# Keys transposed by VectorE instead of TensorE in tiles 1 to 3, diagonal sums moved inside a unit, first loads issued later

## The chip, the core and the metric

The kernel runs on one NeuronCore of a Trainium2 chip. The metric is the device time of one execution in microseconds; the time before is the median of three runs. One execution was profiled, and all rows shown come from it.

## What is computed

One encoder layer over 2048 positions of 1024 channels, in float32. What matters here is its HGRN2 branch: a gated linear recurrence with 4 heads, a 128 x 128 state each, computed chunk by chunk.

```python
h = _rmsnorm(x, mix_norm[l]);  z = h @ w_in[l]
u, v, q, f, i, og, gates = _split_cols(z, IN_SIZES)
...
forget = lb + (1.0 - lb) * sigmoid(ff);  g_log = log(max(forget, TINY));  k = (1.0 - lb) * sigmoid(-ff)
# per chunk, G = cumsum(g_log):
A = einsum('bhid,bhijd,bhjd->bhij', q, decay, k)
o = einsum('bhij,bhje->bhie', A, v) + einsum('bhid,bhde->bhie', q * exp(G), state)
state = exp(G_last) * state + einsum('bhjd,bhje->bhde', k * exp(G_last - G), v)
...
x = x + y @ w_out[l];  x = x + _conv_ffn(_rmsnorm(x, ffn_norm[l]), ...);  return _rmsnorm(x, final_norm)
```

## The kernel before

**Tiling.** The positions are cut into four tiles `t` of 512 (`TT`), each tile into four chunks of 128. Channels lie in the partitions. Weights come in units of 128 output columns; every fp32 product is done as three fp32r products (high weight by high input, high by low, low by high), so that a unit over the eight input blocks is 24 matmuls of 128x512 in `products` (lines 1165, 1166 and 1172). `from_h` is such a unit on the normalised input. In tile 0 each weight unit is loaded raw, split by ScalarE and VectorE (`weights_lo`, line 800), and written out; later tiles load the split units.

**A head.** In each tile, a loop over four heads `h` runs on each engine, and each engine works through its own instructions in the order of the code; semaphores (the `Steps` objects, where `did` counts a step and `at` names the count to wait for) tie them. On TensorE a head is: four units (forget gate, query, gate a, output gate); `level(1)`, two fp32 matmuls of the pair scores at distance 1; two fp32r matmuls with the matrix of ones (lines 1346 and 1348), which sum the diagonal scores into bank 4 and end step `s1`; a fifth unit (gate b); `flip`, four fp32 transposes of the decayed keys `kp` into bank 2 (line 1237, three in the last tile, whose last state is not needed); the levels 2 to 64, twelve fp32 matmuls (line 1245), whose ends are the steps `s2_4`, `s8_16` and `s32_64`; the sixth unit; then the state update (line 1364, keys by token times values), the output products (lines 1369 and 1373) and the mixer (line 1378). Before the update TensorE waits for step `m64` of VectorE, for `k_tok` of ScalarE and for `i_head`.

**VectorE in a head** builds the keys (`kp`, ended by `kl128`) and queries (`qp`, ended by `qp128`, line 931) of all levels, then copies the scores under masks out of PSUM into `scores`: level 1, diagonal, and levels 2 to 64 (lines 941 and 945), each copy behind a wait and a one-element memset (line 939). The last copy is `m64`. It goes on with the first state (line 946), the normalised values `v_head` (line 949) and, when the update is there, the four steps of the state (line 957), for each of which TensorE waits at line 1373. ScalarE copies the flipped keys from bank 2 to `k_tok` (line 619) behind the fifth unit.

**The start.** SP issues all loads in the order of its code: parameters, the first piece of x, the two halves of the first weight unit (line 360, semaphore `half_unit_in`, and line 361), three more pieces of x, the second unit (line 363), the last four pieces, the identity. TensorE first runs 13 warm-up products (line 1297). ScalarE makes the high parts: piece 0 of x, both halves of unit 0 (lines 532 and 534), piece 1 of x, then unit 1 (line 528); VectorE makes the low parts of x (line 784).

Of the kernel before, what the change touches and what calls it, by code (L numbers as in the profile page):

```python
# [6 lines left out]
ACT = mybir.ActivationFunctionType  # L7
ALU = mybir.AluOpType

P = 128  # L10
# [6 lines left out]
NH = 4  # L17
# [105 lines left out]
def build(nc, x_t, w_units, par, masks_in, ident_in, gm_wt, ln_b, gm_bs, out):  # L123
# [145 lines left out]
    N_CONST = 16 * 3  # L269

    tok_act = Steps(sem("tok_act"), ["v0", "v1"] + [f"i{c}" for c in range(NC)])
    head_act = Steps(sem("head_act"), ["i_head", "sig_f", "sig_q", "qk_hi", "sig_og", "k_tok", "o_sq", "sq_hi", "o_rms"])
    head_pe = Steps(sem("head_pe"), ["s1", "k_tok", "s2_4", "s8_16", "s32_64", "update", "o", "mix", "o_sum"])
    names = ["forget", "floor", "qk", "qp1", "qr1"]
    for s in LEVELS:
        names += (["qk_lo"] if s == 16 else []) + [f"kc{s}", f"kl{2 * s}", f"t{2 * s}"]
    for s in LEVELS:
        names += ([f"qr{s}"] if s > 1 else []) + [f"qp{2 * s}"]
    head_dve = Steps(sem("head_dve"), ["k"] + names
                     + ["m1", "m0", "m2", "m4", "m8", "m16", "m32", "m64", "st0"] + [f"vh{c}" for c in range(NC)] + ["st1", "st2", "st3", "st4",  # L280
                        "mix", "sq_lo", "a", "a_hi", "a_lo", "inv", "unit", "b", "b_hi", "b_lo"])
    ln_dve = Steps(sem("ln_dve"), [f"bn{c}" for c in range(NC)] + [f"ag{c}" for c in range(NC)] + ["inv"])
    ln_act = Steps(sem("ln_act"), ["std"])
    mix_dve = Steps(sem("mix_dve"), [f"{n}{j}" for j in range(2) for n in ("b", "a", "y", "y_hi", "y_lo")], 1)
# [69 lines left out]
    def _(sp):  # L354
# [59 lines left out]
        load_x(0, 0)  # L414
        load_raw(0)
        load_x(0, 1)
        load_x(0, 2)
        load_x(0, 3)
        load_raw(1)
# [62 lines left out]
    def _(act):  # L482
# [68 lines left out]
        for t in range(0, NT):  # L551
# [44 lines left out]
            for h in range(0, NH):  # L596
                it = t * NH + h
                u = h * 6
                act.wait_ge(*tok_act.at(f"i{NC - 1}", t))
                act.activation(blocks(i_head[:, :], P), i_tok[:, :, bass.ts(h, P)],  # L600
                               ACT.Copy).then_inc(*head_act.did("i_head"))
                unit_behind(t, U_HEAD, u)
                act.activation(sig_f[:, :], bank[0][:, :], ACT.Sigmoid).then_inc(*head_act.did("sig_f"))
                act.activation(sig_nf[:, :], bank[0][:, :], ACT.Sigmoid, scale=-1.0).then_inc(evac[0], 1)
                unit_behind(t, U_HEAD + 1, u)
                act.activation(sig_q[:, :], bank[1][:, :], ACT.Sigmoid).then_inc(*head_act.did("sig_q"))
                act.wait_ge(*head_dve.at("qk", it))
                act.activation(qk_hi[:, :], qk[:, :], ACT.Copy).then_inc(*head_act.did("qk_hi"))
                unit_behind(t, U_HEAD + 2, u)
                if h == 0 and t:  # L610
                    act.wait_ge(out_sent, t * 16 * KD)
                act.activation(gate_a_head[:, h, :], bank[0][:, :], ACT.Sigmoid).then_inc(evac[0], 1)
                unit_behind(t, U_HEAD + 3, u)
                act.activation(sig_og[:, :], bank[1][:, :], ACT.Sigmoid).then_inc(*head_act.did("sig_og"))
                unit_behind(t, U_HEAD + 4, u)
                act.activation(gate_b_head[:, h, :], bank[0][:, :], ACT.Sigmoid).then_inc(evac[0], 1)
                act.wait_ge(*head_pe.at("k_tok", it))
                tokens = (NC - (t == NT - 1)) * P
                act.activation(k_tok[:, 0:tokens], bank[2][:, 0:tokens], ACT.Copy).then_inc(*head_act.did("k_tok"))
                unit_behind(t, U_HEAD + 5, u)  # L620
                act.activation(u_act[:, h, :], bank[1][:, :], ACT.Gelu).then_inc(evac[1], 1)
                act.wait_ge(*head_pe.at("o", it))
                act.activation(head_o[:, :], bank[4][:, :], ACT.Square).then_inc(*head_act.did("o_sq"))
                act.wait_ge(*head_act.at("o_sq", it))
                act.activation(sq_hi[:, :], head_o[:, :], ACT.Copy).then_inc(*head_act.did("sq_hi"))
                act.wait_ge(*head_pe.at("o_sum", it))
                act.activation(head_o[:, :], bank[5][:, :], ACT.Sqrt, bias=eps[:, 0:1],
                               scale=1.0 / P).then_inc(*head_act.did("o_rms"))
# [90 lines left out]
    def _(dve):  # L719
# [121 lines left out]
        for t in range(0, NT):  # L841
# [25 lines left out]
            for h in range(0, NH):  # L867
# [62 lines left out]
                    then(f"qr{s}")  # L930
                    dve.tensor_tensor(q_r, queries(s), spread(t_l, s), ALU.mult).then_inc(*head_dve.did(f"qp{2 * s}"))

                for n, (s, made, before) in enumerate(((1, "s1", f"qp{P}"), (0, "s1", "m1"), (2, "s2_4", "m0"),
                                                       (4, "s2_4", "m2"), (8, "s8_16", "m4"), (16, "s8_16", "m8"),
                                                       (32, "s32_64", "m16"), (64, "s32_64", "m32"))):
                    dve.wait_ge(*zero_dve.at("scores", t))
                    dve.wait_ge(*head_pe.at(made, it))
                    then(before)
                    dve.memset(scratch[:, n:n + 1], 0.0)
                    if s:  # L940
                        dve.copy_predicated(half_of(scores[:, :], s, True),
                                            mask_of[s].rearrange("p (a n s) -> p a n s", a=2, s=s),
                                            level_out(s).rearrange("p (a n s) -> p a n s", a=2, s=s)).then_inc(*head_dve.did(f"m{s}"))
                    else:
                        dve.copy_predicated(scores[:, :], mask_of[0], bank[4][:, :]).then_inc(*head_dve.did("m0"))
# [210 lines left out]
    def _(pe):  # L1156
# [142 lines left out]
        for t in range(0, NT):  # L1299
# [26 lines left out]
            def o_sum(h):  # L1326
# [3 lines left out]
                pe.wait_ge(*head_dve.at("sq_lo", t * NH + h))  # L1330
                pe.matmul(bank[5][:, :], ones_r[:, :], sq_lo[:, :], start=False, stop=True).then_inc(*head_pe.did("o_sum"))

            for h in range(0, NH):
                it = t * NH + h
                u = h * 6
                used = t * B_TILE + h * 3 + B_HEAD
                from_h(t, U_HEAD, u, 0, used, within=o_sum if h else None, of=h - 1)
                from_h(t, U_HEAD + 1, u, 1, used)
                from_h(t, U_HEAD + 2, u, 0, used + 1)
                from_h(t, U_HEAD + 3, u, 1, used + 1)  # L1340
                pe.wait_ge(*tok_act.at(f"i{NC - 1}", t))
                pe.wait_ge(*head_dve.at("qr1", it))
                pe.wait_ge(*head_dve.at("kc1", it))
                level(1)
                pe.wait_ge(*head_act.at("qk_hi", it))
                pe.matmul(bank[4][:, :], ones_r[:, :], qk_hi[:, :], start=True, stop=False)
                pe.wait_ge(*head_dve.at("qk_lo", it))
                pe.matmul(bank[4][:, :], ones_r[:, :], qk_lo[:, :], start=False, stop=True).then_inc(*head_pe.did("s1"))
                from_h(t, U_HEAD + 4, u, 0, used + 2)
                pe.wait_ge(*head_dve.at(f"kl{P}", it))  # L1350
                flip(bank[2], kp, NC - (t == NT - 1)).then_inc(*head_pe.did("k_tok"))
                for a, b in ((2, 4), (8, 16), (32, 64)):
                    pe.wait_ge(*head_dve.at(f"qr{a}", it))
                    level(a)
                    pe.wait_ge(*head_dve.at(f"qr{b}", it))
                    level(b).then_inc(*head_pe.did(f"s{a}_{b}"))
                from_h(t, U_HEAD + 5, u, 1, used + 2)
                pe.wait_ge(*head_dve.at("m64", it))
                pe.wait_ge(*head_act.at("k_tok", it))
                pe.wait_ge(*head_act.at("i_head", it))  # L1360

                for c in range(NC - (t == NT - 1)):
                    cols = slice(c * P, (c + 1) * P)
                    mm = pe.matmul(bank[2][:, cols], k_tok[:, cols], i_head[:, cols], start=True, stop=True)  # L1364
                mm.then_inc(*head_pe.did("update"))
                for c in range(NC):
                    cols = slice(lain(c) * P, (lain(c) + 1) * P)
                    none_yet = t == 0 and c == 0
                    mm = pe.matmul(bank[4][:, cols], i_head[:, cols], scores[:, cols], start=True, stop=none_yet)  # L1369
                    if none_yet:  # L1370
                        continue
                    pe.wait_ge(*head_dve.at(f"st{c}", it))
                    mm = pe.matmul(bank[4][:, cols], state[:, c, :], qp[:, cols], start=False, stop=True)  # L1373
                mm.then_inc(*head_pe.did("o"))

                for c in range(NC):
                    cols = slice(c * P, (c + 1) * P)
                    mm = pe.matmul(bank[3][:, cols], v_head[:, cols], gm_w[:, h, :], start=True, stop=True)  # L1378
                mm.then_inc(*head_pe.did("mix"))
# [201 lines left out]
```

## Time and profile before

| | us |
|---|---|
| median of 3 runs | 2819.47 |
| lowest, highest | 2819.13, 2820.02 |
| profiled execution, its own time | 2818.25 |
| its span | 2816.4 |
| TensorE busy | 2805.1 (100% of the span) |
| TensorE weight load busy | 2340.2 (83%) |
| VectorE busy | 1562.7 (55%) |
| ScalarE busy | 745.3 (26%) |
| GpSimd busy | 123.0 (4%) |

The granted TensorE clock is full speed in all 40 slices of the span. "PE" is TensorE's matmul side, "PEld" its weight loads, DVE VectorE, ACT ScalarE, POOL GpSimd, SP the engine that issues the loads. Matmuls overlap: a record of 128x512 lasts 0.39 us, while the next one starts 0.227 us after it, so the time that a stretch takes on TensorE is read from start to start. An fp32 matmul leaves two records.

### The profile page before, as it was taken

How to read it: one execution, taken by the hardware profiler on the slowest of the kernel's cores; microseconds unless marked ns; L12 is line 12 of the kernel's file. 1: busy time of each engine (PE TensorE's matmuls, PEld its weight loads, DVE VectorE, ACT ScalarE, POOL GpSimd, SP SyncE). 2: the span in 40 equal slices, each digit the busy share in tenths (PEclk: the TensorE clock that was granted, in tenths of full speed). 3: DMA queues.
4: the chain of work that ended last, by engine and by line, in shares of the span. 5: the costliest groups of instructions: out<-in, count | busy, mean ns of one | idle time of the engine just before them, and what ended most of it. 6: DMA issues, size and time to landing. Idle time of an engine off the chain costs nothing.

```text
span 2816.4 us, 32878 instructions
## 1 busy us (share of the span) xinstructions
PE 2805.1 (100%) x12934; PEld 2340.2 (83%) x12934; DVE 1562.7 (55%) x3044; ACT 745.3 (26%) x1021; POOL 123.0 (4%) x72
## 2 busy tenths in 40 slices
PE   9999999999999999999999999999999999999998
PEld 8888888888888888888888888888888888888887
DVE  6995777756377345553347734555334772555521
ACT  5433344433132113221123201222112220222200
POOL 1003400024000000000000000000000000000000
PEclk9999999999999999999999999999999999999999
DMA  8678888889644555556564455555656445555555
GB/s 313 231 245 280 299 292 290 291 322 319 242 148 163 191 212 194 195 194 233 208 224 147 159 197 207 194 194 194 237 211 215 157 151 212 200 193 192 194 207 177
DMA packets 123739, 614.58 MB, mean 218 GB/s; under 512 B 13987, under 2 KB 16337, under 8 KB 76096
## 3 DMA queue, kind: packets, MB, share of 16 engines
q1 hardware_dynamic: 122688, 610.50, 61.3%
q8 instruction: 103, 1.69, 0.2%
q0 software_dynamic: 896, 1.97, 0.2%
q14 instruction: 52, 0.43, 0.0%
HBM read 474.00 MB, written 138.41 MB: 217 GB/s over the span
## 4 chain that ended last, share of the span: by engine, by line
PE 99%; DVE 1%; DMA 0%; ACT 0%; issue 0%; SPq 0%; DVEq 0%
PE bank L1165 29%; PE bank L1166 29%; PE bank L1172 29%; PE bank L1245 2%; PE bank L1232 2%; PE bank L1230 2%; PE bank L1231 2%; PE bank L1373 1%; PE bank L1279 1%; PE bank L1364 1%; PE bank L1378 1%; PE bank L1369 1%; PE bank L1288 0%; PE bank L1285 0%; PE bank L1181 0%; PE bank L1178 0%
## 5 line engine op out<-in xcount | busy, mean ns | idle before, releaser
L1165 PE MATMUL bank<-h_hi,w_both 128*128 128x512 f32 x2400 | 937.1, 390 | 0.0
L1166 PE MATMUL bank<-h_lo,w_both 128*128 128x512 f32 x2400 | 934.5, 389 | 0.0
L1172 PE MATMUL bank<-h_hi,w_both 128*128 128x512 f32 x2400 | 593.4, 389 | 0.0
L1172 PEld LDWEIGHTS bank<-h_hi,w_both 128*128 128x128 f32 x2400 | 450.5, 188 | 93.4
L1165 PEld LDWEIGHTS bank<-h_hi,w_both 128*128 128x128 f32 x2400 | 450.7, 188 | 93.1
L1166 PEld LDWEIGHTS bank<-h_lo,w_both 128*128 128x128 f32 x2400 | 450.7, 188 | 93.2
L1055 DVE TENSOR_TENSOR z<-bank,rms_inv 128x512 f32<-128x512 f32 x176 | 121.9, 692 | 340.9 <-PE bank L1172 340.6
L1068 DVE SCALAR_TENSOR_TENSOR conv<-z,params,conv 128x512 f32<-128x512 f32 x352 | 263.7, 750 | 6.2
L1166 PE MATMUL bank<-g_lo,w_both 128*128 128x512 f32 x682 | 265.3, 389 | 0.0
L1165 PE MATMUL bank<-g_hi,w_both 128*128 128x512 f32 x682 | 265.3, 389 | 0.0
L493 ACT ACTIVATE w_both<-raw 128x1024 fp32r<-128x1024 f32 x122 | 129.5, 1061 | 325.7 <-PE bank L1172 277.8
L665 ACT ACTIVATE conv<-z,params 128x512 f32<-128x512 f32 x176 | 143.5, 815 | 178.4 <-DVE z L1055 170.2
L1172 PE MATMUL bank<-g_hi,w_both 128*128 128x512 f32 x682 | 169.7, 389 | 0.0
L1165 PEld LDWEIGHTS bank<-g_hi,w_both 128*128 128x128 f32 x682 | 128.0, 188 | 26.6
L1166 PEld LDWEIGHTS bank<-g_lo,w_both 128*128 128x128 f32 x682 | 128.0, 188 | 26.6
L1172 PEld LDWEIGHTS bank<-g_hi,w_both 128*128 128x128 f32 x682 | 128.0, 188 | 26.6
L1121 DVE TENSOR_TENSOR res<-res,bank 128x512 f32<-128x512 f32 x31 | 21.3, 687 | 231.0 <-PE bank L1172 231.0
L479 POOL TENSOR_TENSOR w_both<-raw,w_both 128x1024 fp32r<-128x1024 f32 x46 | 111.2, 2418 | 551.5 <-ACT w_both L493 536.1
L670 ACT ACTIVATE silu<-conv 128x512 f32<-128x512 f32 x88 | 55.4, 630 | 239.4 <-PE bank L1172 232.6
L800 DVE TENSOR_TENSOR w_both<-raw,w_both 128x1024 fp32r<-128x1024 f32 x78 | 95.4, 1223 | 18.8 <-ACT w_both L493 11.9
L674 ACT ACTIVATE g_hi<-g_f 128x512 fp32r<-128x512 f32 x88 | 55.7, 633 | 151.8 <-DVE g_f L1078 151.8
L1165 PE MATMUL bank<-y_hi,w_both 128*128 128x512 f32 x224 | 87.1, 389 | 0.0
(268 smaller groups left out, 3176.6 us busy)
## 6 DMA issues: line engine op xcount, KB each, us to landing
w_both<-w_split SPq DMA_DIRECT2D x371, 1024.0 KB, 4.8
w_split<-w_both SPq DMA_DIRECT2D x248, 512.0 KB, 5.6
raw<-w_units SPq DMA_DIRECT2D x123, 512.0 KB, 5.3
x_in<-x_t SPq DMA_DIRECT2D x32, 256.0 KB, 5.7
res<-x_t SPq DMA_DIRECT2D x32, 256.0 KB, 5.2
out<-res SPq DMA_DIRECT2D x24, 256.0 KB, 7.1
out<-res SPq DMA_DIRECT2D x16, 128.0 KB, 1.9
w_both<-w_split SPq DMA_DIRECT2D x2, 512.0 KB, 5.6
```

The lines of the kernel that those rows point to most:

```text
L479: po.tensor_tensor(w_lo[j], raw[j][:, :, :], w_hi[j].bitcast(F32), ALU.subtract).then_inc(lo_made, 1)
L493: act.activation(w_hi[slot], raw[slot][:, :, :], ACT.Copy).then_inc(hi_made, 1)
L665: act.activation(conv[j][:, :], z[j][:, 2:TT + 2], ACT.Identity, bias=par_col(C_CB + f + j * KF), scale=par_col(C_CW + 4 * KF + f + j * KF ...
L800: dve.tensor_tensor(w_lo[u % 2], raw[u % 2][:, :, :], w_hi[u % 2].bitcast(F32), ALU.subtract).then_inc(lo_made, 1)
L1055: dve.tensor_tensor(z[j][:, 2:TT + 2], bank[2 * (f % 2) + j][:, :], rms_inv[:, :], ALU.mult).then_inc(evac[j], 1)
L1068: dve.scalar_tensor_tensor(out=conv[j][:, :], in0=z[j][:, tap:TT + tap], scalar=par_col(C_CW + 2 * KF * tap + f + j * KF), in1=conv[j][:, ...
L1165: pe.matmul(dst, w_hi[slot][:, off + k, :], rhs_hi(k), start=first and k == 0, stop=False)
L1166: pe.matmul(dst, w_hi[slot][:, off + k, :], rhs_lo(k), start=False, stop=False)
L1172: mm = pe.matmul(dst, w_lo[slot][:, off + k, :], rhs_hi(k), start=False, stop=last and k == n - 1)
L1230: pe.matmul(dst[c][:, :], hi, w[0], start=k == 0, stop=False)
L1231: pe.matmul(dst[c][:, :], hi, w[1], start=False, stop=False)
L1232: mm = pe.matmul(dst[c][:, :], lo, w[0], start=False, stop=k == KD - 1)
```

## The change

Three things are altered.

1. In tiles 1 to 3 the transposes of `kp` are made by VectorE: 16 block transposes of 32 partitions by four times 32 columns (the four chunks at once) write `k_tok` directly, behind `qp128` and ahead of the masked copies. `flip` on TensorE and the copy on ScalarE remain in tile 0 alone. TensorE's wait for `k_tok` ahead of the update goes to the new semaphores.
2. The two diagonal sums are issued in the middle of the fifth unit (`diagonal`, after the first eight matmuls), and `level(1)` goes behind the fifth unit to the other levels. `s1` now ends with the diagonal alone, so the diagonal copy `m0` comes first on VectorE and level 1 (`m1`) waits for `s2_4`.
3. SP waits for `half_unit_in` after the second piece of x; what follows in its queue (pieces 2 and 3, the second unit, pieces 4 to 7, the identity, and all later transfers) is issued behind that wait.

```diff
@@ SP
         load_x(0, 1)
+
+        sp.wait_ge(half_unit_in, 16)
         load_x(0, 2)
@@ ScalarE, head loop
-                act.wait_ge(*head_pe.at("k_tok", it))
-                tokens = (NC - (t == NT - 1)) * P
-                act.activation(k_tok[:, 0:tokens], bank[2][:, 0:tokens], ACT.Copy).then_inc(*head_act.did("k_tok"))
+                if t == 0:
+                    act.wait_ge(*keys_pe.at("flip", h))
+                    act.activation(k_tok[:, :], bank[2][:, :], ACT.Copy).then_inc(*keys_act.did("k_tok"))
@@ VectorE, head loop
+                if t:
+                    then(f"kl{P}")
+                    for a in range(0, P, 32):
+                        for b in range(0, P, 32):
+                            op = dve.transpose(blocks(k_tok[b:b + 32, :], P)[:, :, a:a + 32], blocks(kp[a:a + 32, :], P)[:, :, b:b + 32])
+                    op.then_inc(*keys_dve.did("k_tok"))
+
-                for n, (s, made, before) in enumerate(((1, "s1", f"qp{P}"), (0, "s1", "m1"), (2, "s2_4", "m0"),
+                for n, (s, made, before) in enumerate(((0, "s1", f"qp{P}"), (1, "s2_4", "m0"), (2, "s2_4", "m1"),
@@ TensorE, head loop
+            def diagonal(h):
+                it = t * NH + h
+                pe.wait_ge(*tok_act.at(f"i{NC - 1}", t))
+                pe.wait_ge(*head_act.at("qk_hi", it))
+                pe.matmul(bank[4][:, :], ones_r[:, :], qk_hi[:, :], start=True, stop=False)
+                pe.wait_ge(*head_dve.at("qk_lo", it))
+                pe.matmul(bank[4][:, :], ones_r[:, :], qk_lo[:, :], start=False, stop=True).then_inc(*head_pe.did("s1"))
...
-                pe.wait_ge(*tok_act.at(f"i{NC - 1}", t))
+                from_h(t, U_HEAD + 4, u, 0, used + 2, within=diagonal, of=h)
+                if t == 0:
+                    pe.wait_ge(*head_dve.at(f"kl{P}", it))
+                    flip(bank[2], kp, NC).then_inc(*keys_pe.did("flip"))
                 pe.wait_ge(*head_dve.at("qr1", it))
                 pe.wait_ge(*head_dve.at("kc1", it))
                 level(1)
-                pe.wait_ge(*head_act.at("qk_hi", it))
-                pe.matmul(bank[4][:, :], ones_r[:, :], qk_hi[:, :], start=True, stop=False)
-                pe.wait_ge(*head_dve.at("qk_lo", it))
-                pe.matmul(bank[4][:, :], ones_r[:, :], qk_lo[:, :], start=False, stop=True).then_inc(*head_pe.did("s1"))
-                from_h(t, U_HEAD + 4, u, 0, used + 2)
-                pe.wait_ge(*head_dve.at(f"kl{P}", it))
-                flip(bank[2], kp, NC - (t == NT - 1)).then_inc(*head_pe.did("k_tok"))
...
-                pe.wait_ge(*head_act.at("k_tok", it))
+                pe.wait_ge(*(keys_dve.at("k_tok", it - NH) if t else keys_act.at("k_tok", h)))
```

TensorE in a head of tile 1, from the end of the fourth unit to the levels, before the change (the fifth unit's other matmuls left out):

```order
L1172 MATMUL bank<-h_hi,w_both_50 128x512 x8
L1245 MATMUL bank<-qr_101,k_first_93 128x2x64 x2
L1346 MATMUL bank<-qk_hi,ones_r 128x512
L1348 MATMUL bank<-qk_lo,ones_r 128x512
...
L1172 MATMUL bank<-h_hi,w_both_51 128x512 x8
L1237 MATMUL bank<-ident,kp 128x128 x4
L1245 MATMUL bank<-qr_102,k_first_94 128x2x64 x2
```

The same place after the change:

```order
L1185 MATMUL bank<-h_hi,w_both_50 128x512 x8
...
L1351 MATMUL bank<-qk_hi,ones_r 128x512
L1353 MATMUL bank<-qk_lo,ones_r 128x512
...
L1185 MATMUL bank<-h_hi,w_both_51 128x512 x8
L1258 MATMUL bank<-qr_101,k_first_93 128x2x64 x2
L1258 MATMUL bank<-qr_102,k_first_94 128x2x64 x2
```

The four transposes (L1237) are gone, the two sums stand within the fifth unit, and level 1 stands beside level 2.

VectorE at the end of the queries in the same head, before the change (L931 is `qp128`, L945 the diagonal copy):

```order
L931 TENSOR_TENSOR qp<-qr_107,total_114 128x2x2x64
L939 MEMSET scratch 128x1
L941 COPY_PREDICATED scores<-masks,bank 128x2x128
L939 MEMSET scratch 128x1
L945 COPY_PREDICATED scores<-masks,bank 128x512
L939 MEMSET scratch 128x1
L941 COPY_PREDICATED scores<-masks,bank 128x2x64x2
```

And after it:

```order
L936 TENSOR_TENSOR qp<-qr_107,total_114 128x2x2x64
L943 STREAM_TRANSPOSE k_tok<-kp 32x4x32 x16
L952 MEMSET scratch 128x1
L958 COPY_PREDICATED scores<-masks,bank 128x512
L952 MEMSET scratch 128x1
L954 COPY_PREDICATED scores<-masks,bank 128x2x128
L952 MEMSET scratch 128x1
L954 COPY_PREDICATED scores<-masks,bank 128x2x64x2
```

Sixteen transposes stand ahead of the copies, and the diagonal and level 1 have changed places.

## Rows read from the trace of the kernel before

**Rows 1.** The page, part 4: the chain that ended last, by engine.

```profile
PE 99%; DVE 1%; DMA 0%; ACT 0%; issue 0%; SPq 0%; DVEq 0%
```

**Rows 2.** Timeline, TensorE, tile 1: start, length, instruction; the segment that changes.

```profile
811.24 1.98 PE L1172 MATMUL bank<-h_hi,w_both 128*128 128x512 f32 x8
...
816.68 1.98 PE L1172 MATMUL bank<-h_hi,w_both 128*128 128x512 f32 x8
818.50 0.60 PE L1245 MATMUL bank<-qr,k_first 128*128 128x128 f32 x4
...
824.87 0.60 PE L1237 MATMUL bank<-ident,kp 128*128 128x128 f32 x4
825.30 2.84 PE L1245 MATMUL bank<-qr,k_first 128*128 128x128 f32 x24
827.90 0.47 PE L1165 MATMUL bank<-h_hi,w_both 128*128 128x512 f32 x1
```

**Rows 3.** The same timeline where two ones products already stand within a unit.

```profile
798.07 0.39 PE L1329 MATMUL bank<-sq_hi,ones_r 128*128 128x512 f32 x1
...
798.53 0.39 PE L1165 MATMUL bank<-h_hi,w_both 128*128 128x512 f32 x1
```

**Rows 4.** Timeline, TensorE, a head of the last tile: the three transposes.

```profile
2179.85 0.49 PE L1237 MATMUL bank<-ident,kp 128*128 128x128 f32 x3
2180.18 2.84 PE L1245 MATMUL bank<-qr,k_first 128*128 128x128 f32 x24
```

**Rows 5.** Timeline, TensorE, tile 1: the update and the second state's product.

```profile
833.45 1.05 PE L1364 MATMUL bank<-i_head,k_tok 128*128 128x128 f32 x8
...
835.01 0.42 PE L1373 MATMUL bank<-qp,state 128*128 128x128 f32 x2
```

**Rows 6.** Timeline, VectorE, the same head; in brackets idle before, and the releaser.

```profile
823.04 0.43 DVE L931 TENSOR_TENSOR qp<-qr,total 128x256 f32<-128x256 f32 x1
823.63 0.74 DVE L941 COPY_PREDICATED scores<-masks,bank 128x256 f32<-128x256 uint32 x1 [0.17 <-DVE qp L931]
...
826.48 0.06 DVE L939 MEMSET scratch<- 128x1 f32 x1 [1.21 <-PE bank L1245]
...
829.79 0.45 DVE L941 COPY_PREDICATED scores<-masks,bank 128x256 f32<-128x256 uint32 x1 [0.16 <-DVE scores L941]
...
830.13 0.22 DVE L946 COPY state<-carry 128x128 f32<-128x128 f32 x1
...
834.54 1.11 DVE L957 SCALAR_TENSOR_TENSOR state<-state,total,bank 128x128 f32<-128x128 f32 x3 [3.16 <-PE bank L1364]
```

**Rows 7.** Groups by line and shape, VectorE, 806 to 836 us: busy us, mean ns.

```profile
L957 DVE SCALAR_TENSOR_TENSOR state<-state,total,bank 128x128 f32<-128x128 f32 x3 | 1.0, 347 | 3.2 <-PE bank L1364 3.2
...
L918 DVE TENSOR_TENSOR total<-total 128x128 f32<-128x128 f32 x1 | 0.3, 284 | 0.0
```

**Rows 8.** Timeline, VectorE, tile 0, second head: the last masked copy.

```profile
132.22 0.45 DVE L941 COPY_PREDICATED scores<-masks,bank 128x256 f32<-128x256 uint32 x1
```

**Rows 9.** Timeline, TensorE, the same head: the update behind that copy.

```profile
132.72 1.16 PE L1364 MATMUL bank<-i_head,k_tok 128*128 128x128 f32 x8
```

**Rows 10.** Timeline of the start, SP, ScalarE and VectorE.

```profile
4.03 0.43 SPq L363 DMA_DIRECT2D raw<-w_units  x1
...
5.17 0.63 ACT L532 ACTIVATE w_both<-raw 128x512 fp32r<-128x512 f32 x1
...
9.09 0.75 DVE L784 SCALAR_TENSOR_TENSOR hx_lo<-x_in,params,hx_hi 128x512 fp32r<-128x512 f32 x1 [3.08 <-ACT hx_hi L524]
...
10.91 1.06 ACT L528 ACTIVATE w_both<-raw 128x1024 fp32r<-128x1024 f32 x1 [0.81 <-DMA raw<-w_units]
```

**Rows 11.** Timeline of the start, TensorE: first unit.

```profile
7.10 0.66 PE L1285 MATMUL bank<-w_both,hx_hi 128*128 128x512 f32 x1
...
9.20 0.47 PE L1285 MATMUL bank<-w_both,hx_hi 128*128 128x512 f32 x1
9.89 0.49 PE L1288 MATMUL bank<-w_both,hx_lo 128*128 128x512 f32 x1 [0.22 <-DVE hx_lo L784]
```

More of the change, by code:

```diff
@@ L271, in build @@
     tok_act = Steps(sem("tok_act"), ["v0", "v1"] + [f"i{c}" for c in range(NC)])
-    head_act = Steps(sem("head_act"), ["i_head", "sig_f", "sig_q", "qk_hi", "sig_og", "k_tok", "o_sq", "sq_hi", "o_rms"])
-    head_pe = Steps(sem("head_pe"), ["s1", "k_tok", "s2_4", "s8_16", "s32_64", "update", "o", "mix", "o_sum"])
+    head_act = Steps(sem("head_act"), ["i_head", "sig_f", "sig_q", "qk_hi", "sig_og", "o_sq", "sq_hi", "o_rms"])
+    head_pe = Steps(sem("head_pe"), ["s1", "s2_4", "s8_16", "s32_64", "update", "o", "mix", "o_sum"])
     names = ["forget", "floor", "qk", "qp1", "qr1"]
@@ L279, in build @@
     head_dve = Steps(sem("head_dve"), ["k"] + names
-                     + ["m1", "m0", "m2", "m4", "m8", "m16", "m32", "m64", "st0"] + [f"vh{c}" for c in range(NC)] + ["st1", "st2", "st3", "st4",
+                     + ["m0", "m1", "m2", "m4", "m8", "m16", "m32", "m64", "st0"] + [f"vh{c}" for c in range(NC)] + ["st1", "st2", "st3", "st4",
                         "mix", "sq_lo", "a", "a_hi", "a_lo", "inv", "unit", "b", "b_hi", "b_lo"])
+    keys_pe, keys_act = Steps(sem("keys_pe"), ["flip"]), Steps(sem("keys_act"), ["k_tok"])
+    keys_dve = Steps(sem("keys_dve"), ["k_tok"])
     ln_dve = Steps(sem("ln_dve"), [f"bn{c}" for c in range(NC)] + [f"ag{c}" for c in range(NC)] + ["inv"])
```

## The prediction

> **What bounds the kernel now.** I read the chain of waits first: it is TensorE for 99% of the span [rows 1], so the time changes only by what TensorE executes and by how long it stands still. What the change takes off VectorE or ScalarE is worth nothing by itself, and what it puts there is free as long as TensorE doesn't wait. The next view is the timeline of a head of tile 1, on TensorE [rows 2, 5] and on VectorE [rows 6]. The reader is to see who is early there. VectorE waits 1.21 us for the levels and 3.16 us for the update [rows 6]; TensorE reaches the update at 833.45 [rows 5], while the last masked copy was over at 829.79 + 0.45 = 830.24 [rows 6]. That is a slack of about 3 us, and 1.2 us more within VectorE's wait for the levels. All other heads of tiles 1 to 3 repeat this pattern to a few hundredths. Against this slack stand the 16 new transposes.
>
> **What TensorE is spared.** The segment from the end of the fourth unit to the start of the sixth takes 827.90 - 818.50 = 9.40 us [rows 2]. Afterwards it holds one unit, two ones products and fourteen level matmuls. A unit takes 816.68 - 811.24 = 5.44 us [rows 2]. Two ones products within a unit take 798.53 - 798.07 = 0.46 us [rows 3]. Fourteen level matmuls leave 28 records, as the four transposes (4 records) and twelve levels (24) do now: 827.90 - 824.87 = 3.03 us [rows 2]. The sum is 8.93, so a head gains 0.47 us: 0.43 for the transposes (825.30 - 824.87) and 0.04 for one change less between fp32 and fp32r products. In the last tile only three transposes go, 2180.18 - 2179.85 = 0.33 us [rows 4], and the gain is 0.37. Eight heads by 0.47 and four by 0.37 make **5.24 us**. ScalarE's copy also goes; it lay beside TensorE's work and counts nothing. Level 1 comes later than before; its copy on VectorE now waits for `s2_4`. Today's wait for that step ends 826.48 - 825.30 = 1.18 us after the levels' start [rows 2, 6]; the new levels start at 818.50 + 5.44 + 0.46 = 824.40, with level 1 (0.22) ahead, so the step is there at 825.8, while VectorE with the transposes and the diagonal copy ahead gets to it only at about 829.5.
>
> **What VectorE gets.** No transpose by VectorE is in this trace, so the time T from one to the next has to be bounded. The work is 4 by 32 = 128 elements in each partition. A tensor_tensor of 128 elements takes 284 ns and the scalar_tensor_tensor of line 957 347 ns [rows 7]. Two instructions without a wait overlap: the state copy starts at 830.13 while the copy ahead of it ends at 830.24 [rows 6], so 0.11 us. Three dependent ones at line 957 take 1.11 us [rows 6], a gap of (1.11 - 3 x 0.347) / 2 = 0.035 us between end and start. T thus lies between 0.284 - 0.11 = 0.17 and 0.347 + 0.035 = 0.38 us. I choose within this: each transpose writes another block of 32 partitions than the one before, and no row shows two such instructions overlapping, so I take them one after another, 0.284 + 0.035 = 0.32. A block can also leave only when its 32 columns are in; at (0.43 - 0.284) / 128 = 0.00114 us an element [rows 6, 7] that is up to 0.036 us more, 0.355. I take **T = 0.33 us**, 5.28 us a head.
>
> The Trainium skill has a price of its own. "VectorE: DVE Perf Modes", section "The three transpose paths", gives 311 ns for a VectorE transpose of 128x128 bf16. An estimate from it with the gap above is T = 0.346, and the loss below would be 14 us instead of 11. The same page, "Two Vector instructions with no wait between them", holds an instruction until all earlier ones have finished when its input or output starts in another group of 32 partitions than the last one's. By that rule all sixteen run one after another, which speaks against this change; no row here can show it.
>
> **What lies behind the transposes.** Queued behind them on VectorE are all masked copies, `v_head` and the state. The last query product starts at 823.04, and the next instruction without a wait can start 0.32 later, at 823.36. The copies take 823.63 to 826.48 less the wait of 1.21, which is 1.64, then 0.16 for the semaphore between two copies, then 826.48 to 830.24, which is 3.76 [rows 6]: 5.56 us. The last copy then ends at 828.92 + 16T. TensorE arrives at 833.45 - 0.47 = 832.98. Tile 0 shows the case in which TensorE is late for this very reason: the copy ends at 132.67 [rows 8], the update starts 0.05 later [rows 9] and takes 1.16 instead of 1.05 us [rows 5, 9], since its weights were not loaded ahead. So no stall arises while 16T is under 832.98 - 0.05 - 828.92 = 4.01 us, **T under 0.25 us**. Above it the stall is 16T - 4.01 + 0.11. The state behind it can't make it up: the second state's product already lasts 0.42 rather than 0.39 us [rows 5], directly behind the state's steps. With T = 0.33 the stall is 1.38 us a head, 1.28 in the last tile, where TensorE comes 0.10 later. Less the gain, a head loses 0.91, and twelve heads **10.9 us**. A stall doesn't grow from head to head, as VectorE's next head begins with TensorE's units.
>
> **Tile 0.** The transposes stay. The 0.04 us of the changed order is worth up to 0.2 in four heads, but where the update already waits for the last copy [rows 8, 9] it is lost. I take 0.1.
>
> **The start.** TensorE begins at 7.10, when its warm-up ends; the half unit is there by 5.17 [rows 10, 11], so an earlier half unit brings nothing. Then TensorE stands from 9.20 + 0.23 = 9.43 to 9.89 for the low part of piece 1 [rows 10, 11]. With fewer transfers beside it, piece 1 and the second half come earlier, worth up to 0.46 us. Against it, all that follows in SP's queue moves: the second unit was issued at 4.03 and is now issued behind the wait and two pieces, at about 6. Its arrival (just before 10.91 [rows 10]) ended a wait of ScalarE, and pieces 2 and 3 of x are worked on behind it. If it comes as much later as it is issued, 2 us, up to 1.5 us of that reach TensorE. As the transfers until then share the same bandwidth, I take a small gain of 0.2; bounds -0.46 and +1.5.
>
> **Sum.** 2818.25 (the profiled execution's own time; the span of 2816.4 and 1.85 around it) + 10.9 - 0.1 - 0.2 = 2828.85. The median is 1.22 above the profiled execution: 2830.1.
>
> **The rivals.**
>
> - *The transposes overlap and fit* (T under 0.25). For it speaks that most neighbours on VectorE do overlap and that a plain 128-element operation of 284 ns less 0.11 would leave T at 0.17. Against it, the change of partitions at each step. Then the whole gain stands: 2819.47 - 5.24 - 0.3 = 2813.9, faster by 0.2%. This is the case on the other side; it decides at T = 0.25.
> - *They just miss* (T from 0.25 to 0.30). The stall of 0.1 to 0.9 us a head eats the gain: at T = 0.27 stall and gain are equal, and the time is 2819.
> - *Much slower transposes*, for instance two cycles for a 4-byte element: T = 0.33 + 128 x 0.00114 = 0.48, stall 3.8, loss 3.3 a head, 2859. Nothing in the profile speaks for it but that every VectorE row is of another kind.
> - *The start decides.* If the second unit comes 2 us late, 1.5 us are lost once. It shifts each case by that and no more.
>
> **How the numbers follow.** My forecast, VectorE late at the last copy with T between 0.30 and 0.38, has 0.58; overlapping and fitting 0.20; just missing 0.15; much slower 0.07. The predicted time is 2830. In its own case T from 0.30 to 0.38 gives a loss of (16T - 3.90 - 0.47) x 12, 5.2 to 20.5 us, or 2824.5 to 2840. The fitting case with a start at its better end reaches 2813.5. The range 2813.5 to 2840 leaves out the slow case and the edges. A measurement of this kernel can tell about 0.2% (5.6 us) from no change. The fitting case lies just at that bound, so it gives 0.12 to faster and the rest to the same; the near miss is the same, with 0.01 of faster; of my forecast 0.04 falls below 5.6 us. Faster 0.13, same 0.26, slower 0.61.
>
> **What would show it.** In the profile after: between the fifth and sixth unit one block of level matmuls of 3.03 us and no transposes; the ones products 0.46 us within the fifth unit; sixteen transposes a head, 0.33 us from start to start, 5.3 in all; VectorE no longer waiting for the levels, and hardly for the update; the update on TensorE about 0.05 us behind the last masked copy, some 1.3 us behind the sixth unit's end; a head of tile 1 0.9 us longer than now; no wait at line 1288's place at the start. If the update follows the sixth unit without a gap, T was under 0.25 and the forecast is wrong by its main term. A granted clock below full speed behind the new stalls would make the loss larger; nothing here shows that, as the clock is full in every slice.

## The result: 2832.5 us, 0.47% slower

The changed kernel takes 2832.53 us (median of 6 runs, 2831.41 to 2833.33) against 2819.30 for the kernel before on the same chip. The ratio is 1.0047, with a 95% interval of 1.0037 to 1.0057. The forecast was 2830, with a range of 2813.5 to 2840. The profiled execution took 2831.75 us, its span is 2830.0: 13.6 more than before. Of all executions in this document one, in the run called control, took 3111 us at a granted clock of 0.85, and it counts in no ratio; the others had 0.998 or 0.999.

The page after, busy time by engine and the chain that ended last:

```profile
PE 2804.2 (99%) x12890; PEld 2334.3 (82%) x12890; DVE 1620.2 (57%) x3236; ACT 739.5 (26%) x1009; POOL 123.0 (4%) x72
```

```profile
PE 86%; DVE 11%; issue 1%; DMA 1%; ACT 0%; POOL 0%; DVEq 0%; SPq 0%; POOLq 0%; ACTq 0%
```

VectorE, at 1% of the chain before [rows 1], now has 11%. Its busy time rose by 57.5 us, while the span rose by 13.6. TensorE's waits name the place. The view lists who waited for whom: us in total, times, longest.

```profile
PE bank L1382 <- DVE scores L954: 13.2, 12, 1.4
PE bank L1310 <- DVE ones L766: 1.5, 1, 1.5
PE bank L1298 <- ACT hx_hi L529: 1.2, 1, 1.2
```

L1382 is the state update, L954 a masked copy: twelve waits, one for each head of tiles 1 to 3. The third row is the start. Neither is there before; the second row is, at line 1297.

The timeline of a head of tile 1 after the change, TensorE; it answers to [rows 2, 5]:

```profile
819.20 1.98 PE L1185 MATMUL bank<-h_hi,w_both 128*128 128x512 f32 x8
821.01 0.39 PE L1178 MATMUL bank<-h_hi,w_both 128*128 128x512 f32 x1
...
822.83 0.39 PE L1351 MATMUL bank<-qk_hi,ones_r 128*128 128x512 f32 x1
...
825.12 1.98 PE L1185 MATMUL bank<-h_hi,w_both 128*128 128x512 f32 x8
826.93 3.29 PE L1258 MATMUL bank<-qr,k_first 128*128 128x128 f32 x28
829.98 0.48 PE L1178 MATMUL bank<-h_hi,w_both 128*128 128x512 f32 x1
...
833.70 1.98 PE L1185 MATMUL bank<-h_hi,w_both 128*128 128x512 f32 x8
837.02 1.16 PE L1382 MATMUL bank<-i_head,k_tok 128*128 128x128 f32 x8 [1.34 <-DVE scores L954]
```

And VectorE in the same head; it answers to [rows 6]:

```profile
825.57 0.43 DVE L936 TENSOR_TENSOR qp<-qr,total 128x256 f32<-128x256 f32 x1
825.91 5.04 DVE L943 STREAM_TRANSPOSE k_tok<-kp 32x128 f32<-32x128 f32 x16
831.01 0.06 DVE L952 MEMSET scratch<- 128x1 f32 x1
831.09 0.73 DVE L958 COPY_PREDICATED scores<-masks,bank 128x512 f32<-128x512 uint32 x1
831.98 0.06 DVE L952 MEMSET scratch<- 128x1 f32 x1 [0.17 <-DVE scores L958]
832.33 0.74 DVE L954 COPY_PREDICATED scores<-masks,bank 128x256 f32<-128x256 uint32 x1 [0.29 <-issue]
...
836.52 0.44 DVE L954 COPY_PREDICATED scores<-masks,bank 128x256 f32<-128x256 uint32 x1 [0.16 <-DVE scores L954]
```

From the end of the fourth unit to the start of the sixth it is 829.98 - 821.01 = 8.97 us, 0.43 less than the 9.40 before. The last eight matmuls of a unit take 1.81 us (819.20 to 821.01), so the sixth unit ends at 833.70 + 1.81 = 835.51. The last masked copy ends at 836.52 + 0.44 = 836.96, and the update starts at 837.02, 0.06 behind it. The sixteen transposes take from 825.91 to 831.01, 5.10 us or 0.319 each, the pause behind the last one included. The waits of 1.21 and 3.16 us that VectorE had [rows 6] are gone. In this head a further 0.35 us lies between the memset at 831.98 and its copy at 832.33, of which the row puts 0.29 down to "issue": nothing that the profile shows was waited for. Such a gap falls into this stretch in three of the twelve heads, whose wait is 1.34 to 1.37 us; in the other nine it is 1.01 or 1.02.

The start, after the change: the issue of the second unit, ScalarE's wait for it, and TensorE's wait for the high part of the third piece of x, which ScalarE makes behind that unit [rows 10, 11]:

```profile
5.98 0.43 SPq L366 DMA_DIRECT2D raw<-w_units  x1
```

```profile
11.85 1.06 ACT L533 ACTIVATE w_both<-raw 128x1024 fp32r<-128x1024 f32 x1 [3.14 <-DMA raw<-w_units]
```

```profile
13.66 0.47 PE L1298 MATMUL bank<-w_both,hx_hi 128*128 128x512 f32 x1 [1.17 <-ACT hx_hi L529]
14.36 0.50 PE L1301 MATMUL bank<-w_both,hx_lo 128*128 128x512 f32 x1 [0.22 <-DVE hx_lo L789]
```

The unit is issued 1.95 us later and worked on 0.94 us later. The wait within the first unit is gone, a longer one ahead of the second has come, and the first update stands at 92.60 instead of 91.54, 1.06 later.

**Where the 13.6 us are.** Read in this one execution, the update of the first head stands 1.06 us later than before, that of the last head of tile 0 1.04 later (216.14 against 215.10), that of the very last head 13.04 later (2322.91 against 2309.87). So the start costs 1.06, tile 0 nothing, and the stretch with the twelve heads of tiles 1 to 3 costs 12.0. That includes one new wait of 0.3 us for weights. Such a wait, 0.3 to 1.2 us long, is in five of the twelve profiles, with the change and with its parts taken back.

### The profile page after: what moved, and what is told of

Same layout as the page of the kernel before. It is cut to its first block, busy times and chain, and to the rows that moved or that the text cites. A ratio compares the mean times of both kernels' runs of the same rounds, so it can differ in the third digit from the quotient of the medians.

```text
span 2830.0 us, 32986 instructions
## 1 busy us (share of the span) xinstructions
PE 2804.2 (99%) x12890; PEld 2334.3 (82%) x12890; DVE 1620.2 (57%) x3236; ACT 739.5 (26%) x1009; POOL 123.0 (4%) x72
## 4 chain that ended last, share of the span: by engine, by line
PE 86%; DVE 11%; issue 1%; DMA 1%; ACT 0%; POOL 0%; DVEq 0%; SPq 0%; POOLq 0%; ACTq 0%
PE bank L1178 25%; PE bank L1179 25%; PE bank L1185 25%; DVE k_tok L943 2%; PE bank L1243 2%; PE bank L1245 2%; PE bank L1244 2%; DVE scores L954 1%; DVE qp L936 1%; DVE kp L921 1%; DVE k_first L919 1%; DVE qr L930 1%; PE bank L1382 1%; PE bank L1391 1%; PE bank L1396 1%
## 5 line engine op out<-in xcount | busy, mean ns | idle before, releaser
L805 DVE TENSOR_TENSOR w_both<-raw,w_both 128x1024 fp32r<-128x1024 f32 x78 | 95.4, 1224 | 19.2 <-ACT w_both L498 13.6
L1179 PE MATMUL bank<-y_lo,w_both 128*128 128x512 f32 x224 | 87.2, 389 | 0.0
```

The lines of the kernel that those rows point to most:

```text
L805: dve.tensor_tensor(w_lo[u % 2], raw[u % 2][:, :, :], w_hi[u % 2].bitcast(F32), ALU.subtract).then_inc(lo_made, 1)
L1179: pe.matmul(dst, w_hi[slot][:, off + k, :], rhs_lo(k), start=False, stop=False)
```

## The experiments

My theory was that VectorE ends the last masked copy too late, and nothing else matters but the start. The rivals were the start, the new order of diagonal and level 1, and the new wait or semaphores whatever the transposes take.

**The start undone.**

```diff
         load_x(0, 1)
-
-        sp.wait_ge(half_unit_in, 16)
         load_x(0, 2)
```

> The change without its third part: SP issues all loads without the wait for half_unit_in. Theory (VectorE late at the last masked copy, start a side matter): in the profile of the changed kernel the product that opens the head stage stands 1.06 us later than before, so this run gains 1.0 to 1.1 us on it: span about 2829.0, time about 2831.5, and the stall ahead of each update (1.01 us of idle, 12 times) stays. Rival (the start is a main part of the loss, because all later transfers move): 2827 or less.

Measured: 2830.76 us (ratio 1.0041, 1.0026 to 1.0056), span 2829.2. The first update stands at 91.37 us, 1.23 earlier than with the change, but this execution has a wait of 1.2 us for weights at 713.10, ahead of the heads of tile 1, where the changed kernel's has 0.3. The twelve waits for the scores are 13.2 us, as in the changed kernel. The start is a small part of the loss, as expected.

**The start alone.**

```diff
@@ kernel before
         load_x(0, 1)
+        sp.wait_ge(half_unit_in, 16)
         load_x(0, 2)
```

> The kernel before with SP's wait for half_unit_in behind the second piece of x, nothing else. Theory: the second unit's arrival is late, TensorE waits about 1.2 us for its high part and saves 0.46 at the second block of the first unit: the first head's products stand 1.0 to 1.1 us later, span 2817.4, time about 2820, which a ratio cannot tell from no change. Rival (the later transfers bring back what the start loses, or make it larger): first head's products within 0.3 us of before, or over 2 us later.

Measured: 2820.19 us, ratio 1.0006 (0.9997 to 1.0015), which is no difference by itself; the span is 2818.2. In the trace the first update is at 92.62, and the wait at the second unit is there:

```profile
PE bank L1287 <- ACT hx_hi L526: 0.8, 1, 0.8
```

So the trace shows 1.08 us of loss at the first update; the remaining 0.8 of the span lie later and are not traced to a cause. They are less than the scatter of one kernel: the kernel before took 2817.81 to 2819.89 us beside this run.

The size of the loss scatters too. Four profiles have the late issue and the wait for `m64` ahead of the first update (the changed kernel, this run, and the two with fewer and with in-place transposes below): there the second unit lands between 11.33 and 12.06 us, and the first update stands at 91.91 to 92.75. Four have the issue of before and the same wait: 10.70 to 10.89, and 91.37 to 91.54. The start costs 0.4 to 1.4 us, always a loss.

**The order alone.** The transposes stay on TensorE, ScalarE's copy stays, the start is that of before.

```diff
@@ changed kernel, start undone
-                if t == 0:
-                    act.wait_ge(*keys_pe.at("flip", h))
-                    act.activation(k_tok[:, :], bank[2][:, :], ...)
+                act.wait_ge(*keys_pe.at("flip", it))
+                act.activation(k_tok[:, 0:tokens], bank[2][:, 0:tokens], ...)
-                if t:
-                    ... 16 x dve.transpose(...)
-                if t == 0:
-                    ...
-                    flip(bank[2], kp, NC)
+                flip(bank[2], kp, NC - (t == NT - 1))
```

> The second part of the change alone: diagonal sums within the fifth unit, level 1 behind it, diagonal copy first; the transposes stay on TensorE and the copy on ScalarE in all tiles, the start is that of before. Theory: 0.04 us less a head in tiles 1 to 3 and nothing in tile 0, 0.5 us in all: span about 2815.9, time 2819, no idle of TensorE ahead of the update in tiles 1 to 3. Rival (the later copy of level 1 makes the last masked copy late): TensorE idles ahead of the update and the time is 2822 or more.

Measured: 2819.02 us, ratio 0.9997 (0.9987 to 1.0007). TensorE has no wait ahead of the updates of tiles 1 to 3. The span is 2817.3 instead of the expected 2815.9. Two updates of tile 1, one head apart:

```profile
833.71 1.05 PE L1371 MATMUL bank<-i_head,k_tok 128*128 128x128 f32 x8
```

```profile
874.59 1.05 PE L1371 MATMUL bank<-i_head,k_tok 128*128 128x128 f32 x8
```

A head takes 40.88 us, and 40.84 before (874.29 - 833.45). The rival falls, and my gain of 0.04 us a head falls with it: moving the two sums into the unit and level 1 to the other levels is worth nothing that these runs can tell.

**Ten transposes instead of sixteen.** Two transposes of all 128 partitions and eight of 32; half of the key blocks stay in their own rows.

```diff
-                    for a in range(0, P, 32):
+                    for a in (64, 96):
+                        op = dve.transpose(blocks(k_tok[:, :], P)[:, :, a:a + 32], blocks(kp[:, :], P)[:, :, a:a + 32])
+                    for a in (0, 32):
                         for b in range(0, P, 32):
```

> The changed kernel with 10 transposes a head instead of 16: two of all 128 partitions and eight of 32, which leaves half of the key blocks unmoved, so the states are not the reference's. Theory (slack of 4.0 us a head, 0.319 us a transpose): 3.2 us fit, TensorE doesn't wait ahead of the update and the gain of the removed transposes shows in full, less the 1.06 us of the start: span about 2812.3, time about 2815. Rival (the loss hangs on the new semaphore path or the order, not on the time that the transposes take): time stays near 2832.

Measured: 2815.35 us, ratio 0.9987 (0.9978 to 0.9996), span 2813.8. No wait for the scores is left in TensorE's list. The transposes of a head:

```profile
824.88 0.50 DVE L942 STREAM_TRANSPOSE k_tok<-kp 128x128 f32<-128x128 f32 x2
825.30 2.47 DVE L945 STREAM_TRANSPOSE k_tok<-kp 32x128 f32<-32x128 f32 x8
827.83 0.06 DVE L954 MEMSET scratch<- 128x1 f32 x1
```

They take 2.95 us, within the 4.0 that are free. The first and the last update of tile 1 are at 794.10 and 915.26, so a head takes 40.39 us; before, 792.62 and 915.12 give 40.83. The removed transposes of TensorE are worth 0.45 us a head in tile 1. The loss in the heads hangs on the time that VectorE's transposes take; the new semaphores are still there and make TensorE wait nowhere.

**Sixteen transposes that stay in their rows.** Same size and count, but each writes the 32 partitions that it reads, and four in turn work on the same 32; the keys are not put in their right places.

```diff
-    op = dve.transpose(blocks(k_tok[b:b + 32, :], P)[:, :, a:a + 32], blocks(kp[a:a + 32, :], P)[:, :, b:b + 32])
+    op = dve.transpose(blocks(k_tok[a:a + 32, :], P)[:, :, b:b + 32], blocks(kp[a:a + 32, :], P)[:, :, b:b + 32])
```

> The changed kernel with its 16 transposes of the same size and count, but each writes the 32 partitions that it reads (four in turn on each group of 32), so the blocks are transposed without being moved; the recurrence's states are then not the reference's. Theory 1 (a transpose waits for the one ahead because it writes another group of partitions): within a group they overlap like other neighbours, about 0.20 us from start to start, 12 of 16; the sixteen take about 3.7 us instead of 5.1, which fits into the slack of 4.0: time 2815 to 2817. Theory 2 (0.32 us is what a transpose takes wherever it writes): 5.1 us, time unchanged at 2832.

Measured: 2815.82 us, ratio 0.9988 (0.9979 to 0.9997), span 2813.1, no wait for the scores.

```profile
824.01 3.57 DVE L943 STREAM_TRANSPOSE k_tok<-kp 32x128 f32<-32x128 f32 x16
827.64 0.06 DVE L952 MEMSET scratch<- 128x1 f32 x1
```

Sixteen take 3.63 us here and 5.10 in the changed kernel, for the same work. The durations of the same head in both, minimum, median and maximum in ns, first this run and then the changed kernel:

```profile
L943 DVE STREAM_TRANSPOSE k_tok<-kp x16: 256/260/307, 824.0 to 827.3; 32x128 f32<-32x128 f32 x16
```

```profile
L943 DVE STREAM_TRANSPOSE k_tok<-kp x16: 292/302/309, 825.9 to 830.6; 32x128 f32<-32x128 f32 x16
```

Two neighbours of this run, one by one:

```profile
824.23 0.26 DVE L943 STREAM_TRANSPOSE k_tok<-kp 32x128 f32<-32x128 f32 x1
```

```profile
824.43 0.26 DVE L943 STREAM_TRANSPOSE k_tok<-kp 32x128 f32<-32x128 f32 x1
```

A transpose that follows one in the same rows is recorded with about 260 ns, and the next such one starts 0.193 us after it, before it has ended. One whose rows are not those of the one before is recorded with about 302 ns and starts 0.013 or 0.014 us after the end of that one; in the changed kernel the steps from start to start are 0.305 to 0.320 us. This run has three such changes among its sixteen, the changed kernel fifteen. The difference of 1.47 us a head decides the sign, and it is what separates the forecast from its main rival; for twelve instructions it is 0.12 us each.

The single records also say what "change" means. In the changed kernel the input stays in the same 32 partitions for four transposes and only the output moves, and the steps are the same. The four blocks that stay in place (every fifth of the sixteen) are no exception. So what counts is that the output's rows differ from those of the instruction before, not that a block moves from one group to another. The Trainium skill has the rule in "VectorE: DVE Perf Modes", section "Two Vector instructions with no wait between them": an instruction whose input or output starts in another group of 32 partitions than the last one's is held until all earlier ones have finished. The two runs agree with it.

**The wait moved behind the update.**

```diff
-                pe.wait_ge(*head_dve.at("m64", it))
                 pe.wait_ge(*(keys_dve.at("k_tok", it - NH) if t else keys_act.at("k_tok", h)))
                 ... update ...
+                pe.wait_ge(*head_dve.at("m64", it))
                 ... output products ...
```

> The changed kernel with one line moved: TensorE waits for the last masked copy (m64) behind the state update instead of ahead of it; the update doesn't read the scores. Theory (VectorE's chain itself is the bound: last copy, then v_head for 1.11 us, then the state): the update runs about 1.16 us earlier, but the state still starts when v_head ends, and the second state's product comes at most 0.1 us earlier: gain 0 to 1.2 us in all, time 2831 to 2832.5. Rival (the place of the wait is the cause, and the 0.9 us of the update can be hidden): 12 x 0.9 = 10 us less, 2822.

Measured: 2829.14 us, ratio 1.0036 (1.0022 to 1.0050), span 2827.2: 2.8 us less than the changed kernel, not 0 to 1.2, and far from 10. The waits have moved:

```profile
PE bank L1391 <- DVE state L970: 5.5, 12, 0.5
PE bank L1387 <- DVE scores L954: 2.8, 7, 0.5
```

L1391 is a product with the state, L1387 one with the scores. TensorE comes to the update early and then waits for VectorE twice. The bound is VectorE's chain, not the place of the wait: the rival of 10 us falls. I had the state start when `v_head` ends in both kernels; in the changed kernel it waited for the late update, and started 1.25 us after the end of the last masked copy (838.21 - 836.96), here 1.06 (836.66 - 835.60). That is 0.2 us a head in tiles 1 and 2, next to nothing in tile 3, and 1.5 us in all. The rest of the 2.8 us is not the heads of tiles 1 to 3: 0.4 lie at the start of this execution, 0.6 in tile 0, where the line was moved too, and 0.3 is the wait for weights, which this execution doesn't have.

**Slack made, in all tiles.** `v_head` is computed ahead of the wait for `sig_q`, where VectorE idles; TensorE does the mixer products first, then the update, then waits for `m64`; the sums of squares stand two input blocks later.

```diff
@@ VectorE
                 weights_lo(t, next_lo)
+                ... v_head ...
                 dve.wait_ge(*head_act.at("sig_q", it))
@@ TensorE
                 from_h(t, U_HEAD + 5, u, 1, used + 2)
-                pe.wait_ge(*head_dve.at("m64", it))
+                pe.wait_ge(*head_dve.at("m1", it))
+                ... mixer products ...
                 ... update ...
+                pe.wait_ge(*head_dve.at("m64", it))
                 ... output products ...
```

> The changed kernel with the slack made: v_head is computed on VectorE ahead of the wait for sig_q (1.14 us of idle there), TensorE does the mixer products first, then the update, and waits for m64 only ahead of the output products; the sums of squares stand two input blocks later in the next unit. Theory: the transposes (5.1 us) are then covered, TensorE doesn't idle in the heads of tiles 1 to 3, and the removed transposes show: 0.43 us by 8 and 0.33 by 4 less than before, the start costs 1.06, and tile 0 no longer waits for m64 (up to 1 us): span 2811.5 to 2813, time 2814.5 to 2816. Rival (VectorE is late elsewhere as well, at the state or at the next head): over 2820.

Measured: 2823.07 us, ratio 1.0014 (1.0005 to 1.0023), span 2819.9.

> As the one before (v_head early, mixer first, m64 ahead of the output products), with the start of the kernel before. Theory: another 1.06 us less: span 2810.5 to 2812, time about 2814, ratio to before 0.998. Rival (the early start of loads matters no more once the rest is moved): same as with the changed start.

Measured: 2820.98 us, ratio 1.0008 (0.9999 to 1.0017), span 2818.5. This second run has the start of before. Both missed by 6 us and more: my rival was right that VectorE is late elsewhere, though not at the places that it named. In the run with the start of before, TensorE's waits in tile 1 are down to one of 0.2 us, and there is a new one in tile 0:

```profile
PE bank L1257 <- DVE qr L932: 3.5, 4, 1.1
```

L1257 is a level matmul. In tile 0 VectorE also makes the low parts of the weights and has no idle ahead of `sig_q`, so `v_head` there makes the queries late for the levels. The last update of tile 0 stands at 220.71 us instead of 215.10; 0.9 of that are the mixer products now ahead of it, so tile 0 has become 4.7 us longer.

**Control: the same order with TensorE's transposes.**

> Control: the same reordering (v_head early, mixer first, m64 ahead of the output products, start of before), but with the key transposes left on TensorE and the copy on ScalarE. Theory: only the waits of tile 0 for m64 go, up to 1 us: span 2815.5 to 2816.5, so that the difference to the run with VectorE's transposes is 4.8 us (8 x 0.43 + 4 x 0.33). Rival (the reordering itself makes the gain): within 1 us of the run with VectorE's transposes.

Measured: 2824.23 us, ratio 1.0018 (1.0009 to 1.0027), span 2822.9, with the same 3.4 us of waits for queries in tile 0 and one of 1.1 us for weights. The span is 4.4 us above the run with VectorE's transposes, 3.3 without that one wait. The reordering by itself gains nothing; what gain there is comes from taking the transposes off TensorE.

**Slack made in tiles 1 to 3 only**, tile 0 in the order of the changed kernel, start of before.

```diff
@@ VectorE
+                if t:
+                    values()          # v_head
                 dve.wait_ge(*head_act.at("sig_q", it))
@@ TensorE
+                if t:
+                    pe.wait_ge(*head_dve.at("m1", it))
+                    mixer(it, h)
+                else:
+                    pe.wait_ge(*head_dve.at("m64", it))
                 ... update ...
+                if t:
+                    pe.wait_ge(*head_dve.at("m64", it))
```

> VectorE's transposes with the slack made in tiles 1 to 3 only (v_head ahead of the wait for sig_q, mixer first, m64 awaited ahead of the output products, sums of squares two blocks later), while tile 0 keeps the order of the changed kernel; start of before. In the run that reordered all tiles TensorE had no gap in tile 1 but waited 3.5 us for queries in tile 0, where VectorE has no idle. Theory: those waits go, and what is left is the gain of the removed transposes, 8 x 0.43 + 4 x 0.33 = 4.8 us: span 2811 to 2812.5, time 2813.5 to 2815, ratio to before 0.998. Rival (the new order costs something in tiles 1 to 3 too): 2817 or more.

Measured: 2816.18 us, ratio 0.9991 (0.9982 to 1.0000), span 2813.7. It beats the changed kernel by 16 us, and the kernel before by 3 us, at the edge of what the runs can tell. A head of tile 1, TensorE:

```profile
831.01 1.97 PE L1192 MATMUL bank<-h_hi,w_both 128*128 128x512 f32 x8
832.82 1.05 PE L1358 MATMUL bank<-gm_w,v_head 128*128 128x128 f32 x8
833.71 1.06 PE L1401 MATMUL bank<-i_head,k_tok 128*128 128x128 f32 x8
834.66 0.49 PE L1408 MATMUL bank<-scores,i_head 128*128 128x128 f32 x2
```

The transposes are covered: mixer and update run without a gap. Of the 4.8 us expected, 2.7 came. The output products start 0.95 us after the update instead of 0.89, and their first record lasts 0.49: `m64` still comes a little late. In the last tile, where the update has one matmul less, it is later: the last masked copy, the update and the output products of its third head.

```profile
2267.62 0.44 DVE L963 COPY_PREDICATED scores<-masks,bank 128x256 f32<-128x256 uint32 x1
```

```profile
2267.19 0.83 PE L1401 MATMUL bank<-i_head,k_tok 128*128 128x128 f32 x6
2268.12 0.49 PE L1408 MATMUL bank<-scores,i_head 128*128 128x128 f32 x2
```

The copy ends at 2268.06, and the products start 0.93 us behind the update where they started 0.67 behind it before (2270.03 - 2269.36). Three heads of the last tile lose 0.26 or 0.27 us each in this way, and gain 0.03 instead of 0.33. Over all twelve heads these delays add up to 1.4 us; 0.7 of the missing 2.1 remain untraced.

## Why the prediction was right, point by point

- **The bound and the place.** Right. TensorE waits at the update for the last masked copy, 0.06 us behind its end as tile 0 had shown with 0.05 [rows 8, 9].
- **The transposes' time T.** 0.33 us was assumed and 0.319 measured. That they run one after another, the choice that decided the sign, was right for the reason given: with three changes of rows instead of fifteen, the same sixteen take 0.227 us each, below the limit of 0.25, and there the kernel is faster than before. That the figure is so close is in part luck. Its parts were borrowed from instructions of another kind and missed in opposite directions: 0.284 for the record, which is 0.302, and 0.035 for the pause behind it, which is 0.014.
- **The slack.** 4.01 us was worked out. With T = 0.319 the formula gives a stall of 5.10 - 4.01 + 0.11 = 1.20 us. From the rows, the wait (start of the update less end of the unit) is 1.17 in the nine plain heads, plus 0.10 or 0.11 for the longer update: 1.27.
- **The gain on TensorE.** 0.47 a head was assumed, and the segment is 0.43 shorter (9.40 to 8.97). The part for the transposes was right (also 0.45 with ten transposes); the 0.04 for the order was not there in the run of the order alone.
- **The heads in all.** 10.9 was forecast and 12.0 measured. The stalls add up to 16.3 us (nine of 1.27, three of 1.62) where the forecast has 16.2 (eight of 1.38, four of 1.28). That they agree is luck again: the forecast stall is too long for a plain head, and the gap of 0.35 us in three heads, a term that the sum didn't have, fills it up. What is left is a gain on TensorE of 4.8 instead of 5.2, 0.3 for weights and 0.2 to 0.3 that no term covers.
- **The start.** Wrong in sign: -0.2 assumed, +1.06 measured, within the stated bounds of -0.46 and +1.5. The step that failed is "As the transfers until then share the same bandwidth, I take a small gain". The second unit was issued 1.95 us later, and ScalarE could take it 0.94 us later; half of the delay came through, not none. The wait of 0.22 us for a low part of x, which was to go, has moved to the second unit. The gain at the first unit can't be credited to the change: TensorE was through with it at 12.32 us instead of 13.44, but the second half of the first weight unit, taken by ScalarE at 7.72 in the profile before, came at 6.08 to 7.04 in five other profiles with the start of before, and there TensorE was through at 12.3 to 13.3.
- **Tile 0.** 0.1 was assumed, nothing came. Its updates wait for `m64` [rows 8, 9], the case in which the prediction itself called such a gain lost.
- **The sum.** The profiled execution rose by 13.5 us where 10.6 was forecast: 1.3 from the start, 1.1 from the heads, 0.1 from tile 0, and 0.5 of the span behind the last update, of which 0.1 is the longer update of the last head and the rest is in no term.

## What to carry over

Moving a cheap step from the engine that sets the time (0.43 us here) to one that idles pays only if it fits between what that engine has to wait for and what is waited for on it; add up the borrowing engine's instructions in one head, from the last event that feeds them to the step that others wait for, and compare the sum with the idle in that stretch, not with what a busy share of 55% seems to leave. Count how often VectorE's instructions change their group of 32 partitions from one to the next: sixteen small block moves cost 5.1 us where the same work with three changes costs 3.6. And where a kernel's first tile has another balance than the rest, as here with VectorE full in tile 0, an order that is good for one can be bad for the other.

## What the runs showed of the hardware

- An fp32 VectorE transpose of 32 partitions by 4 x 32 columns is recorded with about 302 ns when its rows differ from those of the instruction before, and about 260 when they don't; the steps from start to start are 0.316 and 0.193 us. Two of 128 partitions take 0.42 us from the first's start to the next instruction (824.88 to 825.30), and so do the first two of the sixteen that stay in their rows: four times the partitions cost no more.
- In the changed kernel, pauses of 0.35 us without a releaser fell into the critical stretch of three of twelve heads. A like pause of VectorE lies between 536 and 543 us, outside any head, in all twelve profiles. The four without VectorE's transposes have no other behind tile 0's heads, the eight with them have two to four more. So they go with the added instructions; their cause wasn't tested.
